# A two-layer backbone step: the down slots' release moved to VectorE, constants loaded in two parts, and three TensorE changes of order

## What is computed

```python
mod = (jax.nn.silu(cond) @ mod_w + mod_b).reshape(cond.shape[0], 6, D_MODEL)
shift_m, scale_m, gate_m, shift_f, scale_f, gate_f = [mod[:, i, None, :] for i in range(6)]
h = rmsnorm(x, norm_mix_g) * (1.0 + scale_m) + shift_m
out, ctx_tensors = mixer_fn(h)
x = x + gate_m * out
h = rmsnorm(x, norm_ffn_g) * (1.0 + scale_f) + shift_f
x = x + gate_f * hier_moe(h, *moe_params)
```

```python
hidden = jax.nn.silu(jnp.einsum('nd,edf->nef', x, w_gate)) * jnp.einsum('nd,edf->nef', x, w_up)
y = jnp.einsum('nef,efd->nd', hidden * combine[:, :, None].astype(hidden.dtype), w_down)
```

## Time and profile before

| | |
|---|---|
| median of 3 runs | 1369.9 us (1368.17 to 1371.55) |
| the profiled execution: its own time | 1374.56 us |
| the profiled execution: span of its instructions | 1372.8 us |
| PE busy | 1258.2 us (92% of the span) |
| VectorE, ACT, POOL busy | 518.7, 298.5, 132.1 us |
| DMA | 344.69 MB, mean 251 GB/s |
| PE in the expert pairs | from 327.2 to 621.6 us in layer 0, and up to 1363.7 us in layer 1, with the layer-1 mixer between |

### The profile page before, as it was taken

The page is one execution under the profiler, slowest core; times in us unless marked ns, Lnnn a source line. Parts: engine busy times, 40 slices in busy tenths (PEclk is TensorE's granted clock), DMA queues, the critical chain, the costliest instruction groups (busy, mean ns, idle before and its releaser), DMA issues. The chain is left out here.

```text
span 1372.8 us, 14624 instructions
## 1 busy us (share of the span) xinstructions
PE 1258.2 (92%) x5786; PEld 705.1 (51%) x5786; DVE 518.7 (38%) x1016; ACT 298.5 (22%) x712; POOL 132.1 (10%) x139
## 2 busy tenths in 40 slices
PE   4999989998899889798999999999999989999896
PEld 1543346445354435244677766776776455444332
DVE  0176666134100002435633646545565541000035
ACT  2122345132121110115121222211232231111112
POOL 0059900000000001001101000000000000000010
PEclk9999999999999999999999999999999999999998
DMA  9749996365889996721322321332235758999994
GB/s 396 307 140 368 376 420 267 147 258 200 339 368 426 424 426 251 307 89 51 123 92 100 132 83 69 131 108 92 77 138 202 306 213 353 416 418 418 424 425 165
DMA packets 35102, 344.69 MB, mean 251 GB/s; under 512 B 3889, under 2 KB 9009, under 8 KB 15793
## 3 DMA queue, kind: packets, MB, share of 16 engines
q1 hardware_dynamic: 22896, 315.37, 56.7%
q0 software_dynamic: 4608, 16.78, 3.1%
q10 hardware_dynamic: 7488, 11.01, 2.3%
HBM read 324.53 MB, written 18.61 MB: 250 GB/s over the span
## 5 line engine op out<-in xcount | busy, mean ns | idle before, releaser
L795 PE MATMUL PS<-ring,hT 128*64 128x512 f32 x736 | 235.3, 620 | 26.6 <-issue 12.1
L603 PE MATMUL PS<-ring,hT 128*128 128x512 f32 x432 | 190.3, 594 | 0.0
L795 PEld LDWEIGHTS PS<-ring,hT 128*64 128x64 f32 x736 | 78.6, 142 | 115.4 <-issue 115.4
L795 PE MATMUL PS<-area,hT 128*64 128x512 f32 x272 | 125.0, 616 | 10.8 <-PEq L949 10.8
L603 PEld LDWEIGHTS PS<-ring,hT 128*128 128x128 f32 x432 | 81.3, 190 | 98.3 <-issue 97.5
L1965 DVE TENSOR_TENSOR area<-area,PS 128x512 f32<-128x512 f32 x16 | 11.0, 688 | 317.7 <-PE PS L795 317.7
L807 PE MATMUL PS<-ring,area 128*64 128x512 f32 x400 | 115.0, 605 | 5.4 <-DMA ring<-moe_w_down 3.8
L988 PE MATMUL PS<-ring 128*128 128x256 f32 x480 | 108.7, 380 | 1.2 <-ACT ring L1426 1.2
L988 PEld LDWEIGHTS PS<-ring 128*128 128x128 f32 x480 | 91.3, 190 | 13.8 <-issue 1.6
L969 PE MATMUL PS<-ring,area 128*128 128x512 f32 x192 | 83.8, 594 | 3.8 <-ACT area L1514 3.8
L988 PE MATMUL PS<-ring,hT 128*128 128x256 f32 x360 | 82.6, 379 | 0.0
(11 more groups left out here) (302 smaller groups left out, 1498.3 us busy)
## 6 DMA issues: line engine op xcount, KB each, us to landing
ring<-moe_w_down SPq DMA_DIRECT2D x25, 2048.0 KB, 20.1
ring<-mod_w SPq DMA_DIRECT2D x24, 2048.0 KB, 11.6
ring<-moe_w_up SPq DMA_DIRECT2D x24, 2048.0 KB, 15.1
ring<-moe_w_gate SPq DMA_DIRECT2D x22, 2048.0 KB, 14.2
ring<-in_w SPq DMA_DIRECT2D x21, 2048.0 KB, 8.2
area<-moe_w_up SPq DMA_DIRECT2D x8, 2048.0 KB, 13.9
area<-moe_w_gate SPq DMA_DIRECT2D x8, 2048.0 KB, 13.0
ring<-out_w SPq DMA_DIRECT2D x7, 2048.0 KB, 8.4
```

Source lines behind the costliest of these rows:

```text
L603: mm = pe.matmul(out, lhs(k), rhs(k), start=n == 0, stop=n == KD - 1)
L795: mm = pe.matmul(PS[64 * e:64 * e + 64, j, :], g[:, k, 64 * e:64 * e + 64], W[e][k], start=k == 0, stop=k == KD - 1)
```

## The change

Five edits are made together:

1. V and C are loaded in two parts. The order of columns in both is changed, so that what is needed first (the modulation biases, the norm gains, the conditioning vectors, the identity matrix, the selector and eps) stands in front: 144 columns of V and 138 of C. The other 768 and 1501 columns are loaded behind the first chunk of `in_w`, under a semaphore of their own, `rest_loaded`. PE, ACT, POOL and DVE each get one wait for it.
2. The three tiles of x are turned after two chunks of `mod_w` rather than three.
3. TensorE's tests of n are turned round: the short branch stands first and the long code in `Else`, and the same for the inner test, whether more than one further unit is needed. The instructions in the branches are the same.
4. `expert_free[2]` of a pair without overflow is raised by VectorE, in its own `Else`, behind a new wait for both halves of the down product. ACT no longer raises it there. With overflow ACT still does.
5. Four unused constants (`C_IOTA4`) go.

```diff
-            sp.dma_start(V[:, :], par).then_inc(par_loaded, 16)
-            sp.dma_start(C[:, :], cst).then_inc(par_loaded, 16)
+            sp.dma_start(V[:, 0:V_EARLY], par[:, 0:V_EARLY]).then_inc(par_loaded, 16)
+            sp.dma_start(C[:, 0:C_EARLY], cst[:, 0:C_EARLY]).then_inc(par_loaded, 16)
             for i, (kind, l, c) in enumerate(STREAM):
+                if i == MODS + 1:
+                    sp.dma_start(V[:, V_EARLY:], par[:, V_EARLY:]).then_inc(rest_loaded, 16)
+                    sp.dma_start(C[:, C_EARLY:], cst[:, C_EARLY:]).then_inc(rest_loaded, 16)
...
             pe.wait_ge(cond_ready, 2)
-            modulation(0, range(3))
+            modulation(0, range(2))
             norm_turn(0)
-            modulation(0, [3])
+            modulation(0, range(2, MODS))
...
                 if n == 7:
+                    pe.wait_ge(rest_loaded, 32)
                     gate_rows(0, (3, 4, 3, 4), [0])
...
-                    with pe.If(n > CAP):
-
+                    with pe.If(n < CAP + 1):
+                        need(pe, ov_pe, a)
+                        pe.sem_inc(ov_pe, da * OVS)
+                    with pe.Else():
                         if p + 1 < PAIRS:
                             pe.wait_ge(gath_copied, 2 * g + 4)
...
                         unit(p, a, b, c, e, W)
-                        with pe.If(n < CAP + OVC + 1):
-                            pe.wait_ge(ov_pe, a + da)
-                            pe.sem_inc(ov_pe, da * (OVS - 1))
-                        with pe.Else():
+                        with pe.If(n > CAP + OVC):
                             with pe.Fori(1, OVS) as u:
...
                                 pe.nop()
+                        with pe.Else():
+                            pe.wait_ge(ov_pe, a + da)
+                            pe.sem_inc(ov_pe, da * (OVS - 1))
                         pe.nop()
-                    with pe.Else():
-                        need(pe, ov_pe, a)
-                        pe.sem_inc(ov_pe, da * OVS)
                     pe.nop()
...
                     with act.Else():
-                        act.sem_inc(expert_free[2], 1)
                         need(act, ov_act, b)
...
                     with dve.Else():
+                        dve.wait_ge(down_mm, 2 * g + 2)
+                        dve.sem_inc(expert_free[2], 1)
                         if direct:
```

More of the change, by code:

```diff
@@ L49 @@
 BIG = 1e30
[L52 to L60, removed]
+C_ID, C_SEL8, C_EPS = 0, 128, 136
+C_EARLY = 138
+C_ONE, C_IOTA, C_UPPER = 138, 266, 330
+C_DF, C_DB, C_MF, C_MB = 458, 586, 714, 842
+C_COS, C_SIN = 970, 1226
+C_POS, C_SEL20 = 1482, 1486
+C_TOK, C_E64, C_STEP, C_LAND, C_TRI = 1506, 1509, 1525, 1535, 1555
+C_DESC, C_EARLIER = 1619, 1623
+C_ALL = 1639
+V_MODB, V_NG, V_COND = 0, 96, 128
+V_EARLY = 144
+V_CB, V_CNG, V_CNB, V_CW = 144, 148, 152, 156
 V_RW, V_RB, V_DEC, V_QKG = 280, 600, 640, 656
@@ L277, in backbone_kernel @@
         iota_cap = C[:, C_IOTA:C_IOTA + CAP]
-        iota4 = C[:, C_IOTA4:C_IOTA4 + 4]
         def slot(i):
@@ L394, in backbone_kernel @@
         early_ready = sem("early_ready")
+        rest_loaded = sem("rest_loaded")
         half_ready, half_sq = sem("half_ready"), sem("half_sq")
@@ L1259, in _ @@
                 act.activation(stat[:, 58 + t % 2:59 + t % 2], stat[:, 57:58], ACT.Sqrt, bias=eps).then_inc(ln_std, 1)
+            act.wait_ge(rest_loaded, 32)
             for t in range(TT):
@@ L1529, in _ @@
             pool.memset(apad, 0.0).then_inc(pad_zero, 1)
-            pool.wait_ge(par_loaded, 32)
+            pool.wait_ge(rest_loaded, 32)
             pool.wait_ge(glu_done, CB)
@@ L1704, in conv_tap @@
                     last[b] = mark(i)
+            dve.wait_ge(rest_loaded, 32)
             for i in range(2):
@@ L2231, in shape_constants @@
         c[32 * j:32 * j + 20, C_SEL20:C_SEL20 + 20] = np.eye(20)
-    c[:, C_IOTA4:C_IOTA4 + 4] = np.arange(4)
     c[:, C_POS] = i + 1
@@ L2261 @@
     rows = [chunks(a["mod_b0"]), chunks(a["mod_b1"])]
-    rows += [chunks(a[n]) for n in ("norm_mix_g0", "norm_ffn_g0", "norm_mix_g1", "norm_ffn_g1",
-                                    "conv_b0", "conv_norm_g0", "conv_norm_b0")]
+    rows += [chunks(a[n]) for n in ("norm_mix_g0", "norm_ffn_g0", "norm_mix_g1", "norm_ffn_g1")]
+    rows.append(_np.stack([a["c_ctx"], a["c"][0]]).reshape(2, KD, P).transpose(2, 1, 0).reshape(P, 2 * KD))
+    rows += [chunks(a[n]) for n in ("conv_b0", "conv_norm_g0", "conv_norm_b0")]
     rows.append(a["conv_w0"].reshape(TAPS, CB, P).transpose(2, 1, 0).reshape(P, CB * TAPS))
-    rows.append(_np.stack([a["c_ctx"], a["c"][0]]).reshape(2, KD, P).transpose(2, 1, 0).reshape(P, 2 * KD))
     for l in range(2):
```

## The result

The changed kernel takes 1362.98 us, the median of 20 executions (1355.08 to 1370.87). The kernel before took 1370.17 us in 20 executions beside them (1364.76 to 1378.12). The ratio is 0.994, with a 95% interval of 0.9924 to 0.9955, so the change is faster. The medians differ by 7.2 us, and the ratio, taken from all executions, makes it 8.2 us (6.2 to 10.4 by the interval). The forecast of 1356.4 was 6.6 us too low; the time lies in the range, near its upper end.

The account below looks back on a forecast made before the run. It took PE's pairs and the late-starting weight transfers as two chains of nearly equal length, the longer one counting. 3.5 + 1.5 + 7 + 1.5 = 13.5 us, from the median 1369.9 to 1356.4; range 1351 to 1364.5.

Parts of the forecast that it names:

- Part 1 and part 2: At the start, constants in two and turns after two chunks: projection earlier, gain 2.2 to 3.9 us, taken as 3.5.
- Part 3, the inner test: At pair 6 of layer 0 the test itself jumps, before PE's wait for its products: 1.6 us less, taken as 1.5.
- Part 3, the second fetch: End of pair 0, layer 0: landing moves into the next block, second fetch not waited for: 3.4 us, plus 2.6 of clock.
- The price of a jump: At pair ends, the long jump costs the same in either order of branches, 5672 ns at pair 0; PE's queue hides some 4 us.
- The cost of the longer test: At 13 pair ends, not-taken test and semaphore add 0.07 + 0.05 us each, 0.8 us for a layer's six or seven.
- Part 4: Down slots released by VectorE: transfers issued 1.8 to 2.0 us earlier; layer 0 taken as 7 us, layer 1 as 1.5.
- rival (d): Expert stages: transfers did not wait for the release, part 4 gives 0, layer 0 gets 4; sum 9, 1361 us; chance 0.05.
- (b): At 13 pair ends the semaphore holds the branch, jumps start 4.4 us later; about 46 us slower, 1416; chance 0.05.
- (a): End of pair 0, layer 0: the second fetch stays, layer 0 gives only 2.0 us; sum 8.5, 1361.4 us; chance 0.24.
- (c): At the pair ends the clock falls behind pauses, up to 2.6 us each; sum 7.0, 1362.9 us; chance 0.08.

Follow-up runs that it names:

- the stall gone alone: The kernel before with one idle semaphore raise on TensorE ahead of layer 0's expert pairs, so every landing lies one instruction further on: 1365.44 us, 0.9957 of before.
- The four pairs of kernels: ACT's against VectorE's release: before 1 and 0.9999; with one idle instruction 0.9957, 0.9966; changed with old outer test 0.9926, 0.9938; changed 0.9934, 0.994.
- three quarters: The changed kernel with ACT's release, moving only three quarters of the columns of each layer 1 expert chunk but the first: 1351.85 us, 0.9848 of before.

## Why the prediction was right or wrong, point by point

**The direction and the main mechanism** held. The gain comes from TensorE's own waits, and most of it from the one stall at the end of pair 0.

**Part 1 and part 2**, forecast 3.5 us: 3.3 between the two traces. Over the five traces at full load with the split constants and the turns after two chunks the projection starts at 34.6 to 36.0, and over the seven without either at 37.2 to 40.1, so 2.9 us is the difference of the means. The first product came at 10.19 rather than near 9: it was only 1.6 us earlier than before, not 2.9. How much of the start reaches the end is not settled. Parts 1 and 2 with the stall gone, and the stall gone alone, both ran at 0.9957; part 1 added 0.12% to one idle instruction; and the changed kernel with ACT's release beats the turned tests alone by 0.25%. That is 0, 1.6 and 3.4 us, each uncertain by 3 to 4 us. The rest of the constants hid behind the projection, as costed.

**Part 3, the inner test**, forecast 1.5 us: 6.73 became 5.02, 1.7 us. Right, and the traces with the inner test as before show 6.4 us and more. In the times it is too small to be told from noise.

**Part 3, the second fetch**, forecast 3.4 us and 2.6 us of clock: 5.00 became 1.39, 3.6 us, and the half clock behind it is gone. One idle instruction alone gains 5.9 us by its ratio and three gain 4.5, near 6.0 or a little under. The mean granted clock agrees. It was 0.9802 over the 20 executions of the changed kernel and 0.9765 to 0.9773 in the three groups of before, and 6.8 us at half clock are 0.0025 of the span. It is not so in all kernels without the stall: two of them stayed at 0.977. The diagnosis from one stall was right. That part 3 removed it was no merit of turned tests: one instruction more ahead of the pairs does it, and part 1 brings one.

**The price of a jump.** The Trainium skill ("Advanced Engine Details and Errata", Control Flow Timing) gives about 108 ns for a compare-and-branch. The 89 ns at 345.2 are near it, for one that is not taken. The long jumps in the changed kernel's trace took 3.3 to 6.3 us, and turning the inner test, which by that figure is worth nothing, gave 1.7 us; the measurement decides. By the rule on a taken branch to a place that isn't loaded ("Runtime: NRT & Kernel Launch" of the Trainium skill, Instruction fetch mechanics) each order of the branches pays the stall once, and the trace agrees. In the changed kernel one fetch, at 348.5 us, lies within the jump of 5363 ns, as one at 353.1 lay within the 5672 ns before.

**The cost of the longer test** was mis-sized in the working and still came out at nothing. I took 0.12 us a pair end. The trace has 0.3 us from the test to the jump (345.2 to 345.5). But the pauses, whose growth the prediction had named as a sign of being wrong, hardly grew: 22.7 / 12 = 1.9 us before, (26.3 - 1.39) / 12 = 2.1 us after, and 24.6 / 12 = 2.05 and 27.1 / 12 = 2.3 us in the two changed kernels with the old order.

**Part 4 is the step that failed.** "VectorE has nothing to do then but wait, so the issue moves" held: SP issues 0.1 us behind PE's end. But its worth did not show: "transfers bound it: I take 7 for layer 0", where rival (d) leaves 4 without the release, and "the gain is 1.5" in layer 1. By the prediction's own figures part 4 was thus worth 13.5 - 9 = 4.5 us. (The 7 was taken from "some 7.5", which is 7.9 by its own numbers, 395.9 less 388.) The four pairs of kernels show no gain, and together leave room for about 1 us. That is the forecast's rival (d) in its price, though not in its reason, as the issue did follow the release. I had read the 6.4 us of waits for weights in one trace as a fixed margin between two chains. In the 13 traces at full load PE is ready for the last down chunk 243.9 to 249.7 us into layer 1's expert stage, and starts on it at 246.7 to 250.8. Both vary by more than the 1.8 us that the release moves. That this is why the release gains nothing is my reading; no run shows it by itself.

**The sum.** Without part 4 it is the 9 of rival (d). The kernel of this rival, the changed one with ACT's release, gained 0.66%, 9.0 us (5.9 to 12.2), and the changed kernel 8.2. That the 9 is met so well is in part luck, as the start's share of it is not confirmed. The two changed kernels with the outer test in its old order gained 0.74% and 0.62%, 10 and 8.5 us. PE's own gains between the two traces are 3.3 + 3.6 + 1.7 and 3.4 us of clock (half of 6.8), less the 2.2 by which the other twelve pauses grew: 9.8 us. The measured gain does not differ from that beyond its interval. Where some of it can be lost is seen in layer 1: PE waits 2.3 to 3.6 us for the last down chunk in 10 of the 13 traces. Whether it is, isn't settled.

**The other rivals.** (b) fell: the jump starts 4.1 us ahead of PE's end, right behind the semaphore. (a) fell with 1.39 us. (c), the clock taking some of it back, came within 0.1 us of the measured time, but not in its way: the start gave its share in the traces, and the clock was higher, not lower. So the range was kept with part 4 wrong: of the 13.5 us, 5.3 to 6.3 did not come.

**What beats both.** The fastest by ratio is the changed kernel with the outer test and the release both as before (0.9926). It can't be told from the changed kernel.

## What to carry to other kernels

Compare two profiled executions only after asking how far single executions spread: here two traces gave 15 us where the medians gave 7. Where an engine stands still behind a long jump and no data is late, add one idle instruction ahead of the landing before changing anything else; here that did most of the work of a larger edit. And moving a release ahead of another engine's store is worth nothing where two chains end within a microsecond or two of each other in varying order, as I read the four pairs (shown is only that it gained nothing, within about 1 us); fewer bytes would have been worth far more (12 us for a quarter of one layer's).

## What the runs showed of the hardware

- The duration of a long jump on TensorE goes with the load of the DMA while it lasts. Of the 64 long jumps in four traces (before, changed, changed with ACT's release, three quarters) those with a DMA share of 0.02 to 0.25 took 3.3 to 3.9 us, those with 0.52 to 0.71 took 4.8 to 5.9, and those with 0.93 and more 5.8 to 6.6. Most of the light ones are the last of a layer, which land elsewhere, but two compare directly: 3.7 and 3.5 us for the first two pair ends of layer 1 with the transfers cut, 5.3 and 6.2 us for the same two at full load. Some 4 us of a jump are covered by the matmuls already queued, so at the light load it costs nothing.
- Releasing a slot earlier made the stall at a landing longer, 7.62 against 5.00 us, as the fetch that PE waits for comes later: 4.2 us behind the end of the jump, where it was 0.8. In all four traces with VectorE's release it starts 3.9 to 4.2 us behind the jump, in the nine with ACT's 0.7 to 1.5. With VectorE's release SP issues the weights' transfers ahead of it, which I take for the reason. In the trace of the release alone, one fetch of instructions (queue q8) lies between 351 and 357 us, behind the jump and ahead of the product at 356.96. With one packet of 0.02 MB it is small, and it shares the engines with 2 MB chunks:

```profile
q8 instruction: 1, 0.02, 1.0%
```

- After a wait of 2.3 us or more for the last down chunk, the products from there to the end took 14.1 us or more in nine of ten traces, and 12.4 us where the wait was 0.84 or 1.29: a wait of over 2 us there was mostly paid for once more in the clock, 1.7 us. The mean granted clock of the 4 us behind the wait was 0.50 to 0.71 in the nine, and 1.00 in the tenth (after 2.87 us) and in the two with the shorter wait.
